# Load order, bias mask, extra small matmuls and delayed sums in a two-block transformer kernel

## The chip, the core and the metric

The kernel runs on one core of a Trainium2 chip. A core has TensorE (PE, matrix products), VectorE (DVE), ScalarE (ACT), GpSimd (POOL) and SyncE (SP, which here only issues transfers), each with a queue of its own, and 16 DMA engines that move data between the chip's memory (HBM) and the on-chip memory. PSUM, in eight banks, takes TensorE's results. The metric is the device time of one execution in microseconds (us); lower is better.

## The reference

One token sequence of 256 rows by 2048 columns, float32, passes through two blocks. What the change touches lies in the first, and in a product that is computed for the second beside it:

```python
def rms_norm(x, g):
    y = xf * lax.rsqrt(jnp.mean(xf * xf, axis=-1, keepdims=True) + NORM_EPS)
    return (y * g).astype(x.dtype)

# first block
xn = rms_norm(h, pre_mix_norm)
proj = xn @ w_in                                   # 2048 x 4608
qa, ka = axial_rope(rms_norm(qa, q_norm)), axial_rope(rms_norm(ka, k_norm))
out_a = global_gqa(qa, ka, va)                     # 8 heads, softmax over 256 keys
out_b = neighbourhood_attn(qb, kb, vb, rel_pos_bias, rows)
    # 8 heads; a key counts only inside a window of 16 columns of a 64-wide grid;
    # scores + rel_pos_bias[head, row distance, column distance]
mix = concat([out_a, out_b]) @ w_o
h = h + rms_norm(mix, post_mix_norm)
m = square(relu(rms_norm(h, pre_mlp_norm) @ w_up)) @ w_down      # 2048 x 8192 x 2048
h = h + rms_norm(m, post_mlp_norm)
...
# second block, first lines
mod = silu(c) @ w_mod + b_mod                      # 2048 x 12288, one row
mod_c = silu(c_ctx) @ w_mod + b_mod
```

The second block then applies a context projection, a gated recurrence, a convolution branch and another MLP of the same size.

## The kernel before

**Pieces and slots.** Every large product streams its weights in pieces of 256 x 512 (512 KB). SP loads a piece into one of four slots of `raw` (`load`, L556: it waits until the low part of the piece four earlier is done). ScalarE writes its rounded high part `whi` (`split`, L641: it waits for the landing, and until TensorE is done with the piece four earlier). VectorE subtracts and writes the low part `wlo` (`split`, L1735). TensorE multiplies each piece in 12 matmuls of 128 x 512 (high x high, high x low, low x high for two halves of the rows and two of the tokens; `chunk`, L1262, the matmul in L1281). The 12 matmuls of a piece are called a slot here, and eight slots a chunk, which fills 512 columns of the result. ScalarE and VectorE work three pieces ahead of TensorE. Between the pieces each engine does other work, which hand-written tables (`extra`, `inserts`) bind to a slot: the same slot number in each engine's own loop.

**Start.** `k_small` holds an identity matrix (`ident`) and ones. TensorE turns (transposes through `ident`) the first gain vector (`turn_vectors`, L1290), then x in eight groups (`x_turn`, L1256); ScalarE and VectorE make high and low parts of each group with the gain applied (`x_high`, `x_low`). Each group's PSUM bank is free again after its low part. The first product is `w_in`, with nine chunks (0 to 8).

**Loads beside the weights.** SP's queue holds, in the order of the program: `k_small`, the first gain, the weight pieces, after piece 4 fourteen small vectors (`vector_loads`), after piece 8 the rotary tables and column mask (`k_early` to `early`), 64 copies of the bias table in HBM (`bias_rows`), and the head gains `q_norm`, `k_norm` broadcast to all partitions (`gqk`), then in chunks 2 and 3 two of the 32 bias loads into `bm` after each piece. ScalarE's queue loads x in two halves.

**Bias mask.** When all of `bm` has landed, GpSimd adds the column mask to it in one operation over 128 x 4096 elements (L2410). VectorE uses `bm` in the attention that follows `w_in`. In chunks 4 to 7 VectorE also normalises and rotates the heads (`rotate`).

**Modulation.** `silu(c) @ w_mod` is not done in slots of its own. VectorE multiplies a piece of `w_mod` by a column of `silu(c)` and adds it to `macc` (L1927, L1930), eight pieces to a block of 512 columns, for c alone or for both c and c_ctx. When the eighth is in, TensorE sums `macc` over the partitions by small matmuls with ones (`mod_sum`, L1386; in the trace 8 for one vector and 16 for both). A plan (`MOD_PLAN`, `AT`) says in which slots of the `w_o` product and of both MLPs the pieces are taken; `MOD_AT` holds them, `SUM_AT` the sums:

```python
SUM_AT.setdefault((name, (a + 1) // 8), {})[(a + 1) % 8] = n_sum   # a: slot of the eighth piece
```

There are three buffers of `macc`; the first product of a block waits for the sum of the block three before. `mod_of_mixer` and `mixer_gains` on VectorE read the finished sums.

## Time and profile before

| | us |
|---|---|
| three runs, median (lowest to highest) | 2971.78 (2967.68 to 2972.05) |
| the profiled execution | 2973.79 |
| its span, first to last instruction | 2972.0 |
| TensorE busy in it | 2857.4 (96%) |
| VectorE, ScalarE, GpSimd busy | 2014.7, 1355.9, 146.9 |
| mean granted TensorE clock | 0.982 of full speed |

TensorE's matmuls overlap, so its busy share counts neighbouring matmuls without a gap. The granted clock has two levels, 1.2 and 2.4 GHz; 1.00 in a row is the higher one throughout. An idle time in brackets at the end of a row is that of the engine just before the operation, with what ended it.

### The profile page before, as it was taken

The numbers are of one execution on the slowest core, as the hardware profiler recorded it, in microseconds if no ns is written. First come the engines' busy times: TensorE is split into PE (matmuls) and PEld (weight loads), VectorE is DVE, ScalarE is ACT, GpSimd is POOL, SyncE is SP. The second block draws the span as 40 slices with busy tenths as digits, with TensorE's granted clock in tenths as the row PEclk, the third lists the DMA queues.
The fourth block names the chain that finished last, engine by engine and source line by source line (L and its number), as shares of the span: only waits on it lengthen the run. The fifth ranks groups of instructions, "written<-read, shape, count | busy, mean of one in ns | idle before, by whom it ended". The sixth has DMA issues, their size and how long they took to land.

```text
span 2972.0 us, 34985 instructions
## 1 busy us (share of the span) xinstructions
PE 2857.4 (96%) x13258; PEld 2370.4 (80%) x13258; DVE 2014.7 (68%) x2263; ACT 1355.9 (46%) x1633; POOL 146.9 (5%) x103
## 2 busy tenths in 40 slices
PE   7998999999999999999999999989979999999997
PEld 6786787888888887787788888888857888888886
DVE  4665779799789787776686487575557754544554
ACT  4446354444443454555444444653434444344442
POOL 0100001010010100000000000000000001010000
PEclk9999999999999999999999999999989999999998
DMA  7661878987878988555666666405547876665653
GB/s 227 198 195 51 277 255 282 320 266 271 286 258 285 324 287 276 177 184 177 202 184 193 194 188 182 131 1 184 190 144 241 275 220 185 193 189 191 188 188 120
DMA packets 322668, 622.52 MB, mean 209 GB/s; under 512 B 27415, under 2 KB 29591, under 8 KB 320919
## 3 DMA queue, kind: packets, MB, share of 16 engines
q1 hardware_dynamic: 319015, 597.96, 63.1%
q10 hardware_dynamic: 3504, 22.55, 2.0%
q8 instruction: 97, 1.59, 0.2%
q14 instruction: 52, 0.43, 0.0%
HBM read 614.14 MB, written 7.24 MB: 209 GB/s over the span
## 4 chain that ended last, share of the span: by engine, by line
PE 83%; DVE 9%; issue 3%; DMA 3%; ACT 2%; SPq 0%; DVEq 0%; POOL 0%; ACTq 0%; POOLq 0%
PE ps L1281 77%; DVE macc L1930 3%; DVE wlo L1741 2%; DMA raw<-w_in 2%; PE ps L1386 1%; PE ps L1256 1%; ACT whi L648 1%; PE ps L1428 1%; PE ps L1646 1%; DVE tcol L2051 1%; PE ps L1628 1%; PE ps L1608 1%; DMA raw<-w_up 0%; DMA raw<-w_o 0%; PE ps L1357 0%
## 5 line engine op out<-in xcount | busy, mean ns | idle before, releaser
L1741 DVE TENSOR_TENSOR wlo<-raw,whi 128x1024 fp32r<-128x1024 f32 x940 | 1171.9, 1252 | 812.0 <-ACT whi L648 807.5
L648 ACT ACTIVATE whi<-raw 128x1024 fp32r<-128x1024 f32 x940 | 995.8, 1060 | 1312.1 <-PE ps L1281 1222.1
L1281 PE MATMUL ps<-whi,hhi 128*128 128x512 f32 x2064 | 811.7, 393 | 1.7 <-DVE hlo L2057 1.2
L1281 PE MATMUL ps<-whi,hlo 128*128 128x512 f32 x2064 | 804.7, 390 | 0.0
L1281 PE MATMUL ps<-wlo,hhi 128*128 128x512 f32 x2064 | 804.3, 390 | 0.0
L1281 PE MATMUL ps<-whi,xhi 128*128 128x512 f32 x1632 | 649.6, 398 | 21.0 <-DVE wlo L1741 16.4
L1281 PE MATMUL ps<-wlo,xhi 128*128 128x512 f32 x1632 | 642.2, 393 | 0.0
L1281 PE MATMUL ps<-whi,xlo 128*128 128x512 f32 x1632 | 641.8, 393 | 0.0
L1281 PEld LDWEIGHTS ps<-whi,hhi 128*128 128x128 f32 x2064 | 388.2, 188 | 83.4 <-DVE hlo L2057 3.1
L1281 PEld LDWEIGHTS ps<-whi,hlo 128*128 128x128 f32 x2064 | 388.0, 188 | 81.6
L1281 PEld LDWEIGHTS ps<-wlo,hhi 128*128 128x128 f32 x2064 | 388.3, 188 | 79.5 <-issue 1.0
L1281 PEld LDWEIGHTS ps<-whi,xhi 128*128 128x128 f32 x1632 | 311.2, 191 | 89.3 <-DVE wlo L1741 14.5
L1281 PEld LDWEIGHTS ps<-whi,xlo 128*128 128x128 f32 x1632 | 310.6, 190 | 66.0
L1281 PEld LDWEIGHTS ps<-wlo,xhi 128*128 128x128 f32 x1632 | 311.2, 191 | 62.9
L1930 DVE SCALAR_TENSOR_TENSOR macc<-mraw,stat,macc 128x512 f32<-128x512 f32 x480 | 350.4, 760 | 4.5
L2428 POOL TENSOR_TENSOR sqrow<-rrow 128x512 f32<-128x512 f32 x64 | 95.2, 1508 | 1192.7 <-ACT rrow L825 1192.7
L2211 DVE SCALAR_TENSOR_TENSOR yT<-uT,cols,yT 128x252 f32<-128x252 f32 (+17 forms) x144 | 52.9, 431 | 0.0
L2403 POOL TENSOR_TENSOR stat<-stat 128x2 f32<-128x2 f32 x11 | 10.8, 985 | 818.0 <-DVE stat L1759 283.2
L1996 DVE TENSOR_TENSOR yrow<-ps,yrow 128x512 f32<-128x512 f32 x48 | 30.9, 686 | 24.2 <-PE ps L1281 24.2
L1628 PE MATMUL ps<-qD,kD 128*128 128x128 f32 x256 | 35.9, 284 | 7.2 <-DVE qD L2287 6.3
L1386 PEld LDWEIGHTS ps<-small,macc 128*128 128x128 f32 x256 | 33.4, 202 | 11.5 <-DVE macc L1930 10.5
L1990 DVE TENSOR_TENSOR hlo<-ps,hhi 128x512 fp32r<-128x512 f32 x64 | 41.0, 682 | 0.0
(280 smaller groups left out, 1548.0 us busy)
## 6 DMA issues: line engine op xcount, KB each, us to landing
raw<-w_in SPq DMA_DIRECT2D x296, 512.0 KB, 4.3
raw<-mlp_w SPq DMA_DIRECT2D x256, 512.0 KB, 3.7
mraw<-w_mod SPq DMA_DIRECT2D x192, 512.0 KB, 6.1
raw<-w_up SPq DMA_DIRECT2D x128, 512.0 KB, 5.1
raw<-w_down SPq DMA_DIRECT2D x128, 512.0 KB, 5.3
raw<-w_o SPq DMA_DIRECT2D x32, 512.0 KB, 5.8
raw<-w_ple_gate SPq DMA_DIRECT2D x32, 512.0 KB, 4.2
raw<-w_out SPq DMA_DIRECT2D x32, 512.0 KB, 4.3
```

The lines of the kernel that those rows point to most:

```text
L648: nc.scalar.activation(whi[:, s % NSLOT], raw[:, s % NSLOT], ACT.Copy).then_inc(hi_done, 1)
L1256: ins = nc.tensor.transpose(ps[:, TB[t % 2], c:c + P], src, ident)
L1281: ins = nc.tensor.matmul(ps[:, bank(par) + th], a[:, kt, th * P:(th + 1) * P], b[:, (s + u) % NSLOT, k], start=(kt == 0 and m == 0), stop= ...
L1386: ins = nc.tensor.matmul(ps[:, MB, n * 8 + 2 * b + v:n * 8 + 2 * b + v + 1], macc[:, v, m % 3, b * P:(b + 1) * P], ones[:, 0:1], start=Tru ...
L1428: ins = nc.tensor.transpose(ps[:, TB[(t0 + h) % 2], a * T + th * P:a * T + (th + 1) * P], sqrow[:, th, f:f + P], ident)
L1628: ins = nc.tensor.matmul(o[:, (2 * hh + n) * P:(2 * hh + n + 1) * P], k[:, hh, n * P:(n + 1) * P], q[:, hh, t * P:(t + 1) * P], start=True ...
L1741: nc.vector.tensor_tensor(wlo[:, s % NSLOT], raw[:, s % NSLOT], whi[:, s % NSLOT].bitcast(F32), ALU.subtract)\
L1930: ins = nc.vector.scalar_tensor_tensor(out=a, in0=w, scalar=x, in1=a, op0=ALU.mult, op1=ALU.add)
L1990: nc.vector.tensor_tensor(hlo[:, kt:kt + 2], ps[:, TB[(t0 + h) % 2]].rearrange("p (a b) -> p a b", a=2), hhi[:, kt:kt + 2].bitcast(F32), A ...
L1996: ins = nc.vector.tensor_tensor(y, ps[:, bank(g) + th], y, ALU.add)
L2211: nc.vector.scalar_tensor_tensor(out=y, in0=tap_part(uT[:, ct], ct, dd, True), scalar=wcol(TAPS // 2 + dd, ct), in1=y, op0=ALU.mult, op1=A ...
L2428: nc.gpsimd.tensor_tensor(sqrow[:, th], rrow[:, th], rrow[:, th], ALU.mult).then_inc(sq_done, 1)
```

## The change

- **First loads.** SP loads x's first half, piece 0, x's second half and the other pieces, in this order. `k_small` and the first gain go to ScalarE's queue.
- **First splits.** ScalarE and VectorE treat the first group of x before piece 0, not after it.
- **Small matmuls.** TensorE issues 12 matmuls of `ident` by `ident` into an unused PSUM bank after the turn of the first gain, and 6 after the second turn of x (`keep_running`). Nobody reads them.
- **Tables spread.** Bias rows after piece 10, head gains after piece 16, `early` after piece 24; the 32 bias loads in chunks 4 and 5.
- **Bias mask.** Off GpSimd; on VectorE in eight operations of 128 x 512, one per slot of chunk 8. Attention waits for all eight.
- **Sums.** `SUM_AT` puts a sum three slots behind its eighth piece (in the `w_o` product at most in its last slot, 31, so its second sum stays where it was). `mod_of_mixer` moves from slot 1 to 4 and `mixer_gains` from 4 to 6 of chunk 24 of the first MLP. The last sum of that MLP falls behind its last chunk, where the program already issued any such sum.

ScalarE, from the start of the program. Before:

```order
L677 DMA res<-x 128x2x1024 x2
L648 ACT_TABLE_LOAD [waits landed0]
L648 ACTIVATE whi<-raw 128x1024 [waits vec_cols]
L687 ACTIVATE xhi<-ps,cols 128x256 [waits t_done]
L687 ACTIVATE xhi<-ps,cols 128x256
```

With the change:

```order
L685 DMA small<-k_small 128x256
L686 DMA vecs<-pre_mix_norm 16x128
L694 ACT_TABLE_LOAD [waits t_done]
L694 ACTIVATE xhi<-ps,cols 128x256 [waits vec_cols]
L694 ACTIVATE xhi<-ps,cols 128x256
L657 ACTIVATE whi<-raw 128x1024 [waits landed0]
```

The table load now waits for the first turn of x, no longer for piece 0.

TensorE, from the start, with the change (before, the turns of x followed the first row directly):

```order
L1297 MATMUL ps<-small,vecs 128x16 [waits gain_in,small_in]
L1321 MATMUL ps<-small 128x128 x12
L1263 MATMUL ps<-small,res 128x128 [waits x_in0]
L1263 MATMUL ps<-small,res 128x128 x3
L1263 MATMUL ps<-small,res 128x128 [waits x_in0]
L1263 MATMUL ps<-small,res 128x128 x3
L1321 MATMUL ps<-small 128x128 x6
L1263 MATMUL ps<-small,res 128x128 [waits t_free,x_in0,acc_free]
```

The 12 stand ahead of the first turn of x.

SP, behind the small vectors (pieces 5 and on). Before:

```order
L560 DMA raw<-w_in 128x2x512 [waits lo_done] x4
L549 DMA early<-k_early 128x576
L550 DMA bias_rows<-rel_pos_bias 64x3720
L551 DMA gqk<-q_norm 128x8x128
L553 DMA gqk<-k_norm 128x2x128
L560 DMA raw<-w_in 128x2x512 [waits lo_done] x8
L577 DMA bm<-bias_rows 64x4x64 [waits bias_copied]
```

With the change:

```order
L566 DMA raw<-w_in 128x2x512 [waits lo_done] x6
L551 DMA bias_rows<-rel_pos_bias 64x3720
L566 DMA raw<-w_in 128x2x512 [waits lo_done] x6
L554 DMA gqk<-q_norm 128x8x128
L556 DMA gqk<-k_norm 128x2x128
L566 DMA raw<-w_in 128x2x512 [waits lo_done] x8
L560 DMA early<-k_early 128x576
L566 DMA raw<-w_in 128x2x512 [waits lo_done] x8
L583 DMA bm<-bias_rows 64x4x64 [waits bias_copied]
```

The head gains now stand between pieces 16 and 17, alone.

TensorE in chunk 3 of the first MLP, around the fourth sum (sqrow: the turn of the hidden rows in slot 3; "..." stands for the other eleven matmuls of a slot). Before:

```order
L1428 MATMUL ps<-small,sqrow 128x128 x3
L1281 MATMUL ps<-whi,xhi 128x512 [waits lo_done]
...
L1281 MATMUL ps<-whi,xhi 128x512 [waits lo_done]
...
L1386 MATMUL ps<-small,macc 128x1 [waits m_mul]
L1386 MATMUL ps<-small,macc 128x1 x7
L1281 MATMUL ps<-whi,xhi 128x512 [waits lo_done]
```

With the change:

```order
L1441 MATMUL ps<-small,sqrow 128x128 x3
L1288 MATMUL ps<-whi,xhi 128x512 [waits lo_done]
...
L1288 MATMUL ps<-whi,xhi 128x512 [waits lo_done]
...
L1288 MATMUL ps<-whi,xhi 128x512 [waits lo_done]
...
L1288 MATMUL ps<-whi,xhi 128x512 [waits lo_done]
...
L1399 MATMUL ps<-small,macc 128x1 [waits m_mul]
L1399 MATMUL ps<-small,macc 128x1 x7
L1288 MATMUL ps<-whi,xhi 128x512 [waits lo_done]
```

The sum stood before slot 5 of the chunk and now stands before slot 7.

The diff:

```diff
--- before.py
+++ after.py
@@ -469,7 +469,8 @@
                     MOD_AT.setdefault((name, a // 8), {})[a % 8] = len(MODQ)
                     MODQ.append((n, r, n_sum, 2 if both else 1, n_ops))
                     n_ops += 4 if both else 2
-                SUM_AT.setdefault((name, (a + 1) // 8), {})[(a + 1) % 8] = n_sum
+                a = min(a + 3, 31) if name == "o" else a + 3
+                SUM_AT.setdefault((name, a // 8), {})[a % 8] = n_sum
                 n_sum += 1
                 if both:
                     n_ctx_sums = n_sum
@@ -527,8 +528,9 @@
 
         @block.sync
         def _(sp):
-            sp.dma_start(small[:], I["k_small"]).then_inc(small_in, 16)
-            sp.dma_start(vecs[0:KT, 0, :], I["pre_mix_norm"][0].rearrange("(b p) -> b p", p=P)).then_inc(gain_in, 16)
+            def half_tokens(h):
+                sp.dma_start(res[:, :, h * (D // 2):(h + 1) * (D // 2)],
+                             rows_of(I["x"][0])[:, :, h * (D // 2):(h + 1) * (D // 2)]).then_inc(x_in[h], 16)
 
             def vector_loads():
                 for gi, group in enumerate(VEC_GROUPS):
@@ -545,13 +547,17 @@
                         sp.dma_start(vecs[r:r + rows, gi, :], src).then_inc(vec_in, 16)
                         r += rows
 
-            def attention_loads():
-                sp.dma_start(early[:], I["k_early"]).then_inc(early_in, 16)
+            def bias_rows_out():
                 sp.dma_start(bias_rows, bass.AP(I["rel_pos_bias"].tensor, 0, [[0, GRID], [1, NB]])).then_inc(bias_copied, 16)
+
+            def head_gains():
                 sp.dma_start(gqk[:, 0:A_Q * HD].rearrange("p (h d) -> p h d", d=HD),
                              bass.AP(I["q_norm"].tensor, 0, [[0, P], [0, A_Q], [1, HD]])).then_inc(gqk_in, 16)
                 sp.dma_start(gqk[:, A_Q * HD:].rearrange("p (h d) -> p h d", d=HD),
                              bass.AP(I["k_norm"].tensor, 0, [[0, P], [0, A_KV], [1, HD]])).then_inc(gqk_in, 16)
+
+            def tables():
+                sp.dma_start(early[:], I["k_early"]).then_inc(early_in, 16)
 
             def load(src, p, s):
 
@@ -582,11 +588,14 @@
                 bias_load(n)
                 bias_load(n + 1)
 
-            chunk(w_in, 0, 0, extra={4: vector_loads})
-            chunk(w_in, 8, NCH, extra={0: attention_loads})
-            for c in (2, 3):
-                chunk(w_in, 8 * c, c * NCH, extra={u: (lambda n=16 * (c - 2) + 2 * u: two_biases(n)) for u in range(8)})
-            with sp.Fori(4, IN1 // NCH) as i:
+            half_tokens(0)
+            chunk(w_in, 0, 0, extra={0: lambda: half_tokens(1), 4: vector_loads})
+            chunk(w_in, 8, NCH, extra={2: bias_rows_out})
+            chunk(w_in, 16, 2 * NCH, extra={0: head_gains})
+            chunk(w_in, 24, 3 * NCH, extra={0: tables})
+            for c in (4, 5):
+                chunk(w_in, 8 * c, c * NCH, extra={u: (lambda n=16 * (c - 4) + 2 * u: two_biases(n)) for u in range(8)})
+            with sp.Fori(6, IN1 // NCH) as i:
                 chunk(w_in, i * 8, i * NCH)
             def mod_load(q):
                 n, r, _, _, _ = MODQ[q]
@@ -673,10 +682,8 @@
                                                scale=gain[:, 2 * g + j:2 * g + j + 1])
                 ins.then_inc(t_hi, 1)
 
-            for h in range(2):
-                act.dma_start(res[:, :, h * (D // 2):(h + 1) * (D // 2)],
-                              rows_of(I["x"][0])[:, :, h * (D // 2):(h + 1) * (D // 2)]).then_inc(x_in[h], 16)
-
+            act.dma_start(small[:], I["k_small"]).then_inc(small_in, 16)
+            act.dma_start(vecs[0:KT, 0, :], I["pre_mix_norm"][0].rearrange("(b p) -> b p", p=P)).then_inc(gain_in, 16)
             gain0 = col("pre_mix_norm")
 
             def x_high(g):
@@ -707,8 +714,8 @@
 
             p0, g0 = plan["in"]
             act.wait_ge(vec_cols, 1)
+            x_high(0)
             split(0, 0)
-            x_high(0)
             x_high(1)
             split(1, 1)
             x_high(2)
@@ -1309,9 +1316,15 @@
             p0, g0 = plan["in"]
             pe.wait_ge(small_in, 16)
             pe.wait_ge(gain_in, 16)
+            def keep_running(count):
+                for n in range(count):
+                    nc.tensor.matmul(ps[:, 7, 0:P], ident, ident, start=True, stop=True)
+
             turn_vectors(0, 1)
+            keep_running(12)
             x_turn(0)
             x_turn(1)
+            keep_running(6)
             chunk(p0, g0, xhi, xlo, inserts={u: (lambda u=u: x_part(u)) for u in range(8)})
             chunk(p0 + 8, g0 + 1, xhi, xlo, inserts={2: other_vectors})
             chunk(p0 + 16, g0 + 2, xhi, xlo)
@@ -1814,8 +1827,8 @@
             assert n0 == 0
             dve.wait_ge(vec_turned, 1)
             nc.vector.tensor_copy(cols[:, 0:KT], ps[:, MB, 0:KT]).then_inc(vec_cols, 1)
+            x_low(0)
             split(0, 0)
-            x_low(0)
             x_low(1)
             split(1, 1)
             x_low(2)
@@ -1866,6 +1879,15 @@
                     nc.vector.tensor_tensor(pj, ra, rb, ALU.add).then_inc(rope_done, 1)
                     dve.wait_ge(rope_done, n + 1)
                 return dict(enumerate([squares, mean_squares, norm_heads, gain, by_cos, lambda: by_sin(0), lambda: by_sin(1), total]))
+
+            def column_mask(u):
+                if u == 0:
+                    dve.wait_ge(bias_in, 16 * ROWS * B_H)
+                    dve.wait_ge(early_in, 16)
+                n = TH * B_H * ROWS // 8
+                b3 = bm[:].rearrange("p t h (a b) -> p (t h a) b", b=GRID)[:, n * u:n * u + n]
+                nc.vector.tensor_tensor(b3, b3, colmask.unsqueeze(1).to_broadcast([P, n, GRID]), ALU.add).then_inc(bias_done, 1)
+            in_extra[8] = {u: (lambda u=u: column_mask(u)) for u in range(8)}
 
             p0, g0 = plan["in"]
             for c in range(IN1 // NCH):
@@ -1902,7 +1924,7 @@
                 nc.vector.tensor_tensor(xlo[:, HEAD_KT[i]], ps[:, 6 + i % 2, 0:T], xhi[:, HEAD_KT[i]].bitcast(F32), ALU.subtract)\
                     .then_inc(o_lo, 1)
 
-            dve.wait_ge(bias_done, 1)
+            dve.wait_ge(bias_done, 8)
             for i in range(NHEAD + 3):
                 if i < NHEAD:
                     score_max(i)
@@ -2065,7 +2087,7 @@
             d_first = c_first + 32
             context_col = lambda g: mod_col("normc", g, mcol[:, 1], modT[:, 0:KT, 1])
             mlp("mlp1", place({0: lambda: post0_res(3), 1: low1(3), 2: low1(4), 3: low1(5), 4: low1(6), 5: low1(7), 6: norm1_mean_square,
-                               c_first + 1: mod_of_mixer, c_first + 4: mixer_gains,
+                               c_first + 4: mod_of_mixer, c_first + 6: mixer_gains,
                                d_first + 8: context_mean_square, d_first + 10: lambda: scaled_row("normc", trow, trow),
                                d_first + 14: lambda: context_col(0),
                                **{d_first + 16 + 2 * g: (lambda g=g: [mod_low("normc", g, xhi, xlo), context_col(g + 1)]) for g in range(7)},
@@ -2404,11 +2426,6 @@
 
             pool.wait_ge(half_set, 1)
             rstd("norm0")
-            pool.wait_ge(bias_in, 16 * ROWS * B_H)
-            pool.wait_ge(early_in, 16)
-            b3 = bm[:].rearrange("p t h (a b) -> p (t h a) b", b=GRID)
-            nc.gpsimd.tensor_tensor(b3, b3, colmask.unsqueeze(1).to_broadcast([P, TH * B_H * ROWS, GRID]), ALU.add)\
-                .then_inc(bias_done, 1)
             for n in range(4):
                 pool.wait_ge(qk_ss, n + 1)
                 nc.gpsimd.tensor_tensor(stat[:, 24:24 + SET], stat[:, 16:16 + SET], stat[:, 128:128 + SET], ALU.pow)\
```

## Rows read from the trace of the kernel before

**Rows 1.** The page: span; busy time, share and instructions of each engine.

```profile
span 2972.0 us, 34985 instructions
PE 2857.4 (96%) x13258; PEld 2370.4 (80%) x13258; DVE 2014.7 (68%) x2263; ACT 1355.9 (46%) x1633; POOL 146.9 (5%) x103
```

**Rows 2.** VectorE's timeline: start, duration, operation, [idle before it].

```profile
131.25 0.82 DVE L1856 TENSOR_TENSOR rota<-proj,early 128x640 f32<-128x640 f32 x1
...
216.92 1.23 DVE L1741 TENSOR_TENSOR wlo<-raw,whi 128x1024 fp32r<-128x1024 f32 x1 [1.49 <-ACT whi L648]
```

**Rows 3.** Who waited for whom, whole span: us in total, times, longest.

```profile
PE ps L1281 <- DVE wlo L1741: 16.4, 8, 4.5
...
PE ps L1386 <- DVE macc L1930: 6.5, 5, 3.9
```

**Rows 4.** Busy time by stretch, granted clock, DMA.

```profile
core 0: us, PE busy (x) PEld busy (x) DVE busy (x) ACT busy (x) POOL busy (x), PEclk, DMA share, GB/s
50.00:60.00 10.00, 9.49 (x34) 7.60 (x35) 5.27 (x5) 5.99 (x7) 0.00 (x0) 0.76 0.83 259
60.00:80.00 20.00, 20.00 (x90) 16.53 (x90) 9.86 (x9) 8.93 (x11) 0.00 (x0) 1.00 0.88 234
100.00:120.00 20.00, 17.29 (x71) 13.88 (x70) 15.27 (x6) 6.33 (x6) 9.03 (x1) 0.91 0.52 166
338.00:346.00 8.00, 8.00 (x26) 6.49 (x26) 1.18 (x2) 1.56 (x5) 0.00 (x0) 0.57 0.76 277
492.00:499.00 7.00, 7.00 (x25) 6.24 (x26) 5.88 (x8) 0.00 (x0) 0.00 (x0) 0.53 0.85 256
868.00:875.00 7.00, 6.95 (x32) 5.58 (x31) 5.08 (x7) 1.06 (x1) 0.00 (x0) 0.76 0.81 278
```

**Rows 5.** Timeline of the start, all engines.

```profile
8.38 1.97 PE L1256 MATMUL ps<-small,res 128*128 128x128 f32 x8
...
11.98 1.28 ACT L648 ACT_TABLE_LOAD   x1 [11.98 <-DMA raw<-w_in]
...
14.24 1.55 ACT L687 ACTIVATE xhi<-ps,cols 128x256 fp32r<-128x256 f32 x4
...
17.26 0.78 PE L1281 MATMUL ps<-whi,xhi 128*128 128x512 f32 x1
```

**Rows 6.** DMA issues, 0 to 120 us: KB each, us to landing.

```profile
gqk<-q_norm SPq DMA_DIRECT2D x1, 512.0 KB, 19.1
...
vecs<-pre_mix_norm SPq DMA_DIRECT2D x1, 8.0 KB, 6.9
```

**Rows 7.** Timelines around three sums: TensorE, and VectorE before the second.

```profile
336.76 2.31 PE L1386 MATMUL ps<-small,macc 128*128 128x1 f32 x16 [0.84 <-DVE macc L1930]
...
486.85 2.34 DVE L1741 TENSOR_TENSOR wlo<-raw,whi 128x1024 fp32r<-128x1024 f32 x2
...
491.90 3.58 PE L1386 MATMUL ps<-small,macc 128*128 128x1 f32 x16 [3.87 <-DVE macc L1930]
...
868.65 1.95 PE L1386 MATMUL ps<-small,macc 128*128 128x1 f32 x16
```

**Rows 8.** Timeline, 29 to 51 us: SP, ScalarE, TensorE.

```profile
29.13 27.31 SPq L560 DMA_DIRECT2D raw<-w_in  x8
...
48.15 1.06 ACT L648 ACTIVATE whi<-raw 128x1024 fp32r<-128x1024 f32 x1 [9.30 <-DMA raw<-w_in]
...
50.51 0.80 PE L1281 MATMUL ps<-whi,xhi 128*128 128x512 f32 x1 [4.47 <-DVE wlo L1741]
```

**Rows 9.** DMA rate from 30 to 50 us, in 40 steps of 0.5 us.

```profile
GB/s 431 446 446 476 115 44 19 31 41 45 32 27 45 43 42 45 20 41 45 41 44 46 17 38 45 36 34 23 48 73 133 280 410 414 418 377 406 381 410 385
```

**Rows 10.** Timeline of GpSimd and TensorE around the bias mask.

```profile
103.30 9.03 POOL L2410 TENSOR_TENSOR bm<-bm,early 128x4096 f32<-128x4096 f32 x1 [61.82 <-DMA bm<-bias_rows]
...
113.47 0.80 PE L1281 MATMUL ps<-whi,xhi 128*128 128x512 f32 x1 [2.71 <-DVE wlo L1741]
```

**Rows 11.** Chain of work that ended last, 100 to 120 us: start, us, what.

```profile
103.78 9.64 DVE wlo L1741
```


## The prediction

> **What bounds the kernel now.** I read the page's busy shares first, then who waited for whom, then the timeline where the change works. TensorE is busy 96% of a span of 2972.0 us [rows 1], in steps of one 512 KB weight piece (a "slot" of 12 matmuls, 2.72 us: one split of 1.23 us on VectorE plus the 1.49 us that it then sits idle [rows 2]). Nothing that leaves those matmuls alone can win more than the idle and slow-clock time around them, so I priced only that. TensorE waited 16.4 us in 8 waits for the low part of a piece and 6.5 us in 5 waits for a modulation product [rows 3]. The granted clock tells a second price: in a stretch the time lost at the lower level is its width times (1 minus the mean granted clock). That is 10 x 0.24 = 2.4 us in 50 to 60, 20 x 0.09 = 1.8 us in 100 to 120, 8 x 0.43 = 3.4 us in 338 to 346, 7 x 0.47 = 3.3 us in 492 to 499 and 7 x 0.24 = 1.7 us in 868 to 875 [rows 4]. Each follows one of the waits or sums below.
>
> **Start.** Before, the two halves of x and four weight pieces share the DMA engines, the table load waits until piece 0 lands at 11.98, and split, x parts and low parts follow one another to the first product at 17.26 [rows 5]. The change puts x and the weights in one queue in the order of use, and k_small and the first gain in ScalarE's. The new chain does not begin at piece 0 but at that gain, which landed 6.9 us after its issue [rows 6], just ahead of the turns at 8.38 [rows 5]. Then come the 12 new matmuls, which are on the path. No row shows them. Above, the turns at the start take 1.97 / 8 = 0.25 us each [rows 5], so 3.0 us in all; below, the 16 small matmuls of a sum take 1.95 us, 0.12 each, so 1.5 us [rows 7]. With 0.25 (they start after an idle stretch like those turns): turn of the gain to 8.5, 12 matmuls to 11.5, four turns (1.0) to 12.5, table load (1.28) to 13.8, the first pair of high parts (1.55 / 2) to 14.6, split (1.06, as ScalarE's of any piece) to 15.6, low part (1.23) to 16.9: 0.4 us earlier than 17.26. With 0.12 it is 1.9 us earlier. A gain vector that is alone in its queue could land up to 3 us sooner, or the 12 matmuls could cost more than they fill; I take **1.5 us**, between -1 and +5. The matmuls may also lift the clock before the first slot, which runs slow now (up to 1.8 us, the price of the slow stretch after 113); there are still gaps of a microsecond in between, so I count **0.5 us**. The six matmuls after the second turn stand before a wait for VectorE and cost nothing; if that wait were gone, 0.7 to 1.5 us.
>
> **Tables spread.** At 50.51 TensorE stood 4.47 us, and ScalarE 9.30 us for the landing of piece 9 [rows 8]. That piece was issued at 29.13 behind both head gains [rows 8], which take 19.1 us to land [rows 6]; from 32.5 to 44.5 the DMA engines move 17 to 48 GB/s in every half microsecond, from 46 on 400 again [rows 9]. So the broadcast of the gains blocks the queue for 13 us, piece 9 lands 3.1 us after its end (48.1), and 2.4 us later TensorE starts. That is 18.5 us after the gains begin to move, then, against 14.0 us from their begin (32.0) to the need at 50.51 - 4.47 = 46.0: 4.5 us late, as seen. Stall and slow clock (2.4 us, less 0.3 of it inside the stall: 2.1) cost 6.6 us. The change does not take the broadcast away; it puts it after piece 16, with the bias rows no longer before it. It should begin 2 to 3.5 us after its issue, which is 19.5 us before piece 17 is needed (a piece's own lead of 46.0 - 29.1 = 16.9 us, and one slot). That gives 16.0 to 17.5 us where 18.5 are wanted: 1.0 to 2.5 us of stall, now at piece 17, plus about 1.5 us of slow clock behind it. I take 2.0 + 1.5 = 3.5 us, a **gain of 3.1 us** (0 if the stall stays as it is, 6.6 if it goes). Bias rows and the tables, alone among pieces, hide in the same lead. The 32 bias loads go from chunks 2 and 3 to 4 and 5: 60 to 80 shows what they cost beside the weights, TensorE 20.00 of 20.00 with DMA at 0.88 [rows 4], so nothing; SP's pieces queue behind them as before. The new cover is VectorE's rotation, which takes 0.82 us of its 1.49 idle us [rows 2]; without that cover every late piece would be seen.
>
> A rule weighs against this part. The trace says that the 512-byte packets of the broadcast crawl [rows 9]. The Trainium skill, page "DMA: Bandwidth & Descriptors", section Specifications, gives 512 B or more as the smallest transfer for line rate; by that the two gains would pass in about 2 us, the bytes ahead of piece 9 would be to blame, and spreading them would win all 6.6 us. The row decides for me; the rule's case is the third rival.
>
> **Bias mask.** GpSimd's one addition over 4096 elements runs 103.30 to 112.33, and TensorE then waits 2.71 us for VectorE [rows 10]: the split that began at 103.78 lasted 9.64 us [rows 11] in place of 1.23. With the 1.8 us of slow clock, less 0.3 inside the stall, that is **4.2 us**, and it goes entirely. The eight additions of 512 elements on VectorE stand in chunk 8, after the bias loads: 0.82 us for 640 elements [rows 2] makes 0.66 each, 5.3 in all, inside an idle of 1.49 us per slot. Nothing is queued behind them but the splits, three slots ahead of TensorE. If an eighth took GpSimd's rate (1.13 us) it would still fit. Between 3 and 4.5 us.
>
> **Sums two slots later.** A sum of 8 or 16 matmuls stood one slot behind its last product, and TensorE waited for that product although the next piece was ready. At 336.76 it waited 0.84 and lost 3.4 us of clock; at 491.90 it waited 3.87 and lost 3.3 [rows 4, 7]. Two more slots are 5.4 us of room, more than any wait. All five waits go: 6.5 us [rows 3]. The last, about 0.5, is not won: the pieces after it wait for a DMA. At 491.90 VectorE is itself full, and TensorE soon needs its next low part: 0.4 us come back. The clock losses behind the two long ones (6.7) go as well, since there is no idle stretch before them. **12.3 us.** I leave the 1.7 us behind the sum at 868.65 out, which came after 1.95 us of small matmuls and no wait to speak of [rows 4, 7]: the same may now strike one sum of another phase, so it neither goes nor comes. Ends: 5 us (waits alone, part of them found again as waits for low parts) and 15 us. The mixer's modulation and gains, moved by three and two slots on VectorE, are four short operations with a chunk to spare: nothing. No product waits for a later sum, since its buffer is asked for two groups on.
>
> A rule that bears on the 6.7 us: by the Trainium skill, page "TensorE: Matmul & The Clock Gate", section Part 1: The HAM clock gate, the number of slow matmuls at a start differs between runs of the same kernel. By that the 6.7 could be anything from 0 to 8; the first rival has its lower end.
>
> **Sum.** 1.5 + 0.5 + 3.1 + 4.2 + 12.3 = 21.6 us. The profiled execution took 2973.79 us, 2.0 above the median of 2971.78, so 2952.2 for it and **2950.2 for the median**; I say 2950.
>
> **Rivals.**
> 1. The clock does not come back and the start gains nothing: the 16 small matmuls themselves bring the lower level, as at 868.65, wherever they stand. For it: that row. Against: of the six sums of that length that waited under 0.1 us, only that one shows it. 21.6 - 6.7 - 2.0 = 12.9 us: 2959. Chance 0.2.
> 2. The waits for sums turn into waits for low parts, because VectorE is full in 484 to 492. For it: it works without a pause there. Against: two low parts lay ready from 489.2 on [rows 7]. The 3.87 and 3.3 us are lost: 14.4 us, 2957. Chance 0.08.
> 3. The broadcast is not what holds piece 9; its stall goes whole, and the early gain comes 3 us sooner: 21.6 + 3.5 + 3 = 28.1 us, 2944. For it: by bytes alone the queue would be empty at once. Against: [rows 9]. Chance 0.13.
> 4. Slower: the bias loads in chunks 4 and 5 meet the rotation. DMA is busy at 0.88 there and a slot's loads fill the slot; if they took 4.5 us in place of 2.7, sixteen slots would lose 29 us and outweigh the gains: 2979. It decides from 1.4 us lost a slot on (21.6 / 16), with nothing else failing. Against it: the same bytes in 60 to 80 delay nobody. Chance 0.02.
> 5. The change works only in part and ends within 0.2% (about 6 us, what a measurement of this kernel can tell from no change): 0.04.
>
> The forecast itself has 0.53, from 2946 to 2956. The range for 8 in 10 takes in most of rivals 1 to 3: 2942 to 2960. Faster by over 0.2% (below 2965.8): 0.94; within: 0.04; slower: 0.02.
>
> **What would show it.** First product between 14 and 17 us, and its spacing tells the clock. A stall of 1 to 2.5 us at the second piece of chunk 2, none at piece 9. No split above 1.3 us near 103, and eight additions of about 0.66 us with no wait on TensorE in the last chunk. No wait of a sum for macc anywhere, and a full granted clock behind 340 and 490. The forecast is wrong if a stall of over 5 us stands at piece 17, if the waits on macc return as waits on wlo, or if the start moves past 18 us.

## The result, and the profile after

| | before | with the change |
|---|---|---|
| median of four runs each, us | 2969.73 (2966.61 to 2972.05) | 2947.93 (2947.61 to 2951.75) |
| ratio of the times | | 0.9929, interval 0.9914 to 0.9945 |
| profiled execution, us | 2973.79 | 2947.61 |
| its span, us | 2972.0 | 2945.7 |

The change is worth 21.8 us, with an interval of 16 to 26; 21.6 were forecast. The two traces differ by more, 26.3 us of span, because the profiled execution of before is 4.1 us above its median of four, and that of after 0.3 below its own.

The page of the changed kernel: span, and busy time of each engine, to be held against [rows 1].

```profile
span 2945.7 us, 35013 instructions
...
PE 2845.1 (97%) x13294; PEld 2364.0 (80%) x13294; DVE 2013.6 (68%) x2271; ACT 1355.3 (46%) x1633; POOL 139.9 (5%) x102
```

TensorE has 36 matmul records more, two for each of the 18 small matmuls, and is yet busy 12.3 us less: that part was time at the lower clock. The other 14 of the 26.3 us of span are idle time of TensorE that is gone. GpSimd gives up 7 us, VectorE takes eight more instructions.

Who waited for whom in the changed kernel (us in total, times, longest), against [rows 3]:

```profile
PE ps L1288 <- DVE wlo L1754: 13.7, 9, 5.3
```

There is no row of TensorE waiting for macc at L1399 any more (before 6.5 us in 5 waits). Waits for low parts fell from 16.4 to 13.7 us only, because new ones came.

Busy time and granted clock by stretch (columns as in [rows 4]) of the changed kernel. The last three are the stretches around the sums that stood at 336.76, 491.90 and 868.65 before; all work there now comes 12 to 23 us earlier.

```profile
18.00:22.00 4.00, 4.00 (x12) 3.13 (x11) 4.00 (x6) 2.58 (x4) 0.00 (x0) 0.57 0.52 148
44.00:54.00 10.00, 10.00 (x47) 8.12 (x46) 3.76 (x4) 5.16 (x6) 0.00 (x0) 1.00 0.65 207
60.00:80.00 20.00, 17.77 (x78) 14.36 (x78) 7.84 (x7) 7.54 (x10) 0.00 (x0) 1.00 0.67 224
100.00:120.00 20.00, 20.00 (x90) 16.57 (x89) 10.96 (x12) 8.58 (x9) 2.08 (x1) 1.00 0.86 231
326.00:334.00 8.00, 8.00 (x45) 6.92 (x44) 6.87 (x9) 4.33 (x7) 0.00 (x0) 1.00 0.87 301
479.00:486.00 7.00, 7.00 (x40) 6.10 (x40) 6.93 (x10) 2.44 (x3) 0.00 (x0) 1.00 0.86 271
852.00:859.00 7.00, 7.00 (x40) 6.11 (x39) 6.41 (x8) 2.75 (x3) 3.06 (x2) 1.00 0.80 277
```

Each stretch that ran at 0.53 to 0.91 in [rows 4] is at 1.00, with one new loss at 18 to 22. The 40 matmul records in seven microseconds (25 before, at 492) say the same.

**Where the time went.** A difference between two traces can be split by the start of the same piece on TensorE in both timelines. Pieces are counted from 0 within each product, "chunk 4, piece 1" from 0 within the chunk:

| first matmul of | before | after | ahead by | what lies between |
|---|---|---|---|---|
| piece 0 | 17.26 | 17.70 | -0.44 | the start |
| piece 10 | 56.06 | 49.68 | 6.38 | stall at piece 9 and slow clock: +6.82 |
| piece 18 | 77.95 | 74.16 | 3.79 | new stall at piece 17: -2.59 |
| chunk 4, piece 1 | 123.09 | 114.96 | 8.13 | bias mask: +4.34 |
| `w_o`, piece 2 | 293.27 | 284.01 | 9.26 | attention, clock at other places: +1.13 |
| first MLP, chunk 24, piece 1 | 969.24 | 946.17 | 23.07 | sums: +13.81 |
| last piece | 2945.69 | 2919.43 | 26.26 | the rest: +3.19 |

The last row is not a work of the change. It is made of places where the lower clock falls in one trace and not in the other, and of a wait for a transfer in the context projection that takes back about a microsecond.

### The profile page after: what moved, and what is told of

It is laid out like the page before. It is cut to its first block, busy times and chain, and to the rows that moved or that the text cites. A ratio compares the mean times of both kernels' runs of the same rounds, so it can differ in the third digit from the quotient of the medians.

```text
span 2945.7 us, 35013 instructions
## 1 busy us (share of the span) xinstructions
PE 2845.1 (97%) x13294; PEld 2364.0 (80%) x13294; DVE 2013.6 (68%) x2271; ACT 1355.3 (46%) x1633; POOL 139.9 (5%) x102
## 4 chain that ended last, share of the span: by engine, by line
PE 87%; DVE 6%; DMA 3%; issue 2%; ACT 2%; DVEq 0%; SPq 0%; POOL 0%; ACTq 0%; POOLq 0%
PE ps L1288 81%; DVE wlo L1754 1%; DMA raw<-w_in 1%; DVE macc L1952 1%; PE ps L1441 1%; PE ps L1263 1%; PE ps L1399 1%; DMA raw<-w_up 1%; ACT whi L657 1%; PE ps L1641 1%; PE ps L1621 1%; DVE tcol L2073 1%; PE ps L1659 1%; DMA raw<-w_o 0%; PE ps L1370 0%
## 5 line engine op out<-in xcount | busy, mean ns | idle before, releaser
L1288 PE MATMUL ps<-whi,xhi 128*128 128x512 f32 x1632 | 645.1, 395 | 18.3 <-DVE wlo L1754 13.7
L1141 ACT ACTIVATE dec<-ps 128x1024 f32<-128x1024 f32 x32 | 32.4, 1027 | 17.0 <-PE ps L1621 15.1
```

The source lines that it names most:

```text
L1141: nc.scalar.activation(dst, src, ACT.Exp).then_inc(d_done, 1)
L1288: ins = nc.tensor.matmul(ps[:, bank(par) + th], a[:, kt, th * P:(th + 1) * P], b[:, (s + u) % NSLOT, k], start=(kt == 0 and m == 0), stop= ...
```

## The experiments

All were timed beside runs of the kernel before on the same chip, 4 to 11 runs each. Mask alone, mask and tables, sums alone and the change without small matmuls share one series of the kernel before (median 2970.03, 15 runs), the other four a second one on another chip (2969.21, 15 runs). The change itself was timed in a third one.

| kernel | median us | ratio to before | interval |
|---|---|---|---|
| mask alone, on before | 2964.78 | 0.998 | 0.997 to 0.9989 |
| mask and tables spread, on before | 2962.04 | 0.9972 | 0.996 to 0.9984 |
| sums alone, on before | 2955.49 | 0.9948 | 0.9934 to 0.9961 |
| the change without small matmuls | 2943.26 | 0.9903 | 0.9888 to 0.9918 |
| mask in eight parts, still on GpSimd | 2966.62 | 0.9989 | 0.998 to 0.9998 |
| the change, sums two slots behind | 2950.19 | 0.9928 | 0.9915 to 0.9942 |
| the change, head gains in five transfers | 2946.2 | 0.9919 | 0.9905 to 0.9932 |
| the best of these together | 2938.2 | 0.9889 | 0.9874 to 0.9905 |

### The mask alone, and the mask in eight parts on GpSimd

Kernel before, with the change's `column_mask` on VectorE only:

```diff
+            in_extra[8] = {u: (lambda u=u: column_mask(u)) for u in range(8)}
...
-            dve.wait_ge(bias_done, 1)
+            dve.wait_ge(bias_done, 8)
...
-            nc.gpsimd.tensor_tensor(b3, b3, colmask.unsqueeze(1).to_broadcast([P, TH * B_H * ROWS, GRID]), ALU.add)\
-                .then_inc(bias_done, 1)
```

> The kernel before with the bias mask alone moved to VectorE, in eight parts in chunk 8. My theory: GpSimd's 9.03 us addition held VectorE's split (9.64 us in place of 1.23), so both the 2.71 us wait of TensorE near 113 and the 1.5 us of slow clock behind it go: 4.3 us less, no split above 1.3 us near 103, eight additions of 0.66 us. Rival: the split was long because its high part or a transfer was late, and then a long split stays near 103 and nothing is won. A second rival, that VectorE's extra 5.3 us in chunk 8 delay low parts, would give a wait of TensorE after 207.

And the rival form: the addition stays on GpSimd, but cut into eight (VectorE waits for all eight, as above):

```diff
-            nc.gpsimd.tensor_tensor(b3, b3, colmask.unsqueeze(1).to_broadcast([P, TH * B_H * ROWS, GRID]), ALU.add)\
-                .then_inc(bias_done, 1)
+            for u in range(8):
+                n = TH * B_H * ROWS // 8
+                nc.gpsimd.tensor_tensor(b3[:, n * u:n * u + n], b3[:, n * u:n * u + n], colmask.unsqueeze(1).to_broadcast([P, n, GRID]), ALU.add)\
+                    .then_inc(bias_done, 1)
```

> The kernel before with the bias mask still on GpSimd, but cut into eight additions of 512 elements. My theory: a VectorE split that meets a GpSimd addition waits until that one ends; the whole one took 9.03 us, an eighth some 1.1 to 1.3, so a split takes at most 2.5 us, VectorE's lead of 5.6 us covers it, and TensorE's wait near 113 goes: 1.7 to 4.3 us less, as with the mask on VectorE. Rival: it is the total of GpSimd's work beside VectorE that counts, or GpSimd's eight parts follow each other so closely that a split waits for several; then a split of over 7 us and a wait of TensorE stay.

The mask alone gave 5.3 us by the medians (2970.03 - 2964.78), with an interval of 3 to 9 us; its trace gives 2.88 + 1.45 = 4.33 between the same pieces. With eight parts on GpSimd it was 2.6 us by the medians (2969.21 - 2966.62), with an interval of 0.6 to 5.9, and 4.33 by the trace too. VectorE's timeline of the changed kernel, in the last chunk of `w_in`, shows what it costs:

```profile
202.87 0.68 DVE L1889 TENSOR_TENSOR bm<-bm,early 128x512 f32<-128x512 f32 x1
203.47 1.22 DVE L1754 TENSOR_TENSOR wlo<-raw,whi 128x1024 fp32r<-128x1024 f32 x1
204.61 0.68 DVE L1889 TENSOR_TENSOR bm<-bm,early 128x512 f32<-128x512 f32 x1
206.07 1.23 DVE L1754 TENSOR_TENSOR wlo<-raw,whi 128x1024 fp32r<-128x1024 f32 x1 [0.78 <-ACT whi L657]
```

The addition takes 0.68 us and the split behind it still waits for its high part: it fits. With eight parts on GpSimd, the timeline of GpSimd and VectorE reads:

```profile
102.45 14.99 POOL L2412 TENSOR_TENSOR bm<-bm,early 128x512 f32<-128x512 f32 x8 [61.15 <-DMA bm<-bias_rows]
...
108.48 2.07 DVE L1741 TENSOR_TENSOR wlo<-raw,whi 128x1024 fp32r<-128x1024 f32 x1 [1.42 <-ACT whi L648]
111.20 1.59 DVE L1741 TENSOR_TENSOR wlo<-raw,whi 128x1024 fp32r<-128x1024 f32 x1 [0.65 <-ACT whi L648]
113.92 2.36 DVE L1741 TENSOR_TENSOR wlo<-raw,whi 128x1024 fp32r<-128x1024 f32 x1 [1.13 <-ACT whi L648]
116.21 1.92 DVE L1841 TENSOR_TENSOR rota<-proj 128x640 f32<-128x640 f32 x1
```

Splits last up to 2.36 us in place of 1.23, but none 9.64 as in [rows 11], and TensorE does not wait. GpSimd pays too: the same 4096 elements take 14.99 us where the single operation took 9.03 [rows 10]. So the two engines hold each other up, each for about the rest of the other's operation (a split of at most 1.23 + 9.03 / 8 = 2.36 us), and what hurts TensorE is the length of the single operation, not the engine that has it.

The Trainium skill, page "SBUF — State Buffer", section "SBUF: two separate sides", says that VectorE, in an operation with two inputs in SBUF as the split is, and a GpSimd operation that reads SBUF share a pair of ports as an exclusive lock held for the whole instruction. The rows agree. Even the order in time fits: in the kernel with the sums alone, the split was there first.

```profile
103.98 1.23 DVE L1742 TENSOR_TENSOR wlo<-raw,whi 128x1024 fp32r<-128x1024 f32 x1 [1.49 <-ACT whi L649]
104.58 9.55 POOL L2411 TENSOR_TENSOR bm<-bm,early 128x4096 f32<-128x4096 f32 x1 [63.17 <-DMA bm<-bias_rows]
...
106.71 8.50 DVE L1742 TENSOR_TENSOR wlo<-raw,whi 128x1024 fp32r<-128x1024 f32 x1 [1.50 <-ACT whi L649]
```

There the first split ran its normal 1.23 us, GpSimd's operation took 9.55 in place of 9.03, and the next split was held for 8.50. TensorE then waited 1.59 us, at 115.27, and its clock stayed at 1.00 from 100 to 120. Between piece 18 and chunk 4, piece 1, this comes to 1.9 us in this trace and 4.3 in that of before, so the price of the mask varies between traces. That it varies with where in a slot the addition begins is likely, but two traces don't show it.

### The tables spread, beside the mask

```diff
-            chunk(w_in, 8, NCH, extra={0: attention_loads})
-            for c in (2, 3):
-                chunk(w_in, 8 * c, c * NCH, extra={u: (lambda n=16 * (c - 2) + 2 * u: two_biases(n)) for u in range(8)})
-            with sp.Fori(4, IN1 // NCH) as i:
+            chunk(w_in, 8, NCH, extra={2: bias_rows_out})
+            chunk(w_in, 16, 2 * NCH, extra={0: head_gains})
+            chunk(w_in, 24, 3 * NCH, extra={0: tables})
+            for c in (4, 5):
+                chunk(w_in, 8 * c, c * NCH, extra={u: (lambda n=16 * (c - 4) + 2 * u: two_biases(n)) for u in range(8)})
+            with sp.Fori(6, IN1 // NCH) as i:
```

(and the edits of the mask kernel). The spread was not tried without the mask: with the bias loads in chunks 4 and 5, GpSimd would wait for them ahead of the steps that the rotation in chunk 4 needs, while the loads wait for the pieces behind that rotation.

> The mask on VectorE and the tables spread as in the change; start and sums as before. Against the mask alone this shows the spreading: my theory gives 6.8 us won at piece 9 (4.6 wait, 2.2 slow clock) and 2.2 to 2.4 us lost at piece 17, where the head gains now stand in front; so about 4.4 us less than the mask alone, 8.7 less than before. Rival: the gain at piece 9 needs the new start too (x and weights in one queue), and then a wait of some us stays at piece 9.

2962.04, 2.7 us below the mask alone, where 4.4 were expected; the intervals of the two ratios overlap. Its trace has the 4.63 and 2.15 us won at pieces 9 and 10, so the new start is not needed for them, and a new wait of 1.49 us at piece 17 (69.20). From piece 8 to 18 the traces give 4.9 us against the mask alone; why the medians show less was not traced. In the changed kernel the same wait at piece 17 is 2.23. Its path runs through three timelines; SP, ScalarE and TensorE:

```profile
49.30 0.47 SPq L554 DMA_DIRECT2D gqk<-q_norm  x1
49.81 0.97 SPq L556 DMA_DIRECT2D gqk<-k_norm  x1
...
68.90 1.06 ACT L657 ACTIVATE whi<-raw 128x1024 fp32r<-128x1024 f32 x1 [9.58 <-DMA raw<-w_in]
...
71.27 0.50 PE L1288 MATMUL ps<-whi,xhi 128*128 128x512 f32 x1 [2.23 <-DVE wlo L1754]
```

and the DMA rate of the changed kernel from 48 to 75 us (40 steps of 0.675 us), with the share of time in which its DMA engines were busy, in tenths, and the time to landing of the gains:

```profile
DMA  4795677312210111331122222499999987317896
GB/s 46 246 394 149 146 303 266 105 54 49 56 56 24 44 42 45 28 35 39 42 55 70 84 74 83 149 322 387 408 361 361 355 340 285 143 33 146 313 337 164
...
gqk<-q_norm SPq DMA_DIRECT2D x1, 512.0 KB, 16.8
gqk<-k_norm SPq DMA_DIRECT2D x1, 128.0 KB, 17.7
```

From 53 to 65 us the DMA engines again move 24 to 84 GB/s, and piece 17 lands behind it at 68.9. So the broadcast itself is slow, wherever it stands, as the prediction read from [rows 9]. The engines were busy under four tenths of that time, mostly one or two: in the DMA records of the trace a 512-byte packet of the broadcast holds its engine for 25 ns in the median and a 2048-byte packet of a weight piece for 84, so the time goes between the packets and not in them. What the move changed is how early it is issued against the need.

### The head gains in five transfers

The changed kernel, with the broadcast cut by heads and spread over pieces:

```diff
-            chunk(w_in, 16, 2 * NCH, extra={0: head_gains})
-            chunk(w_in, 24, 3 * NCH, extra={0: tables})
+            chunk(w_in, 16, 2 * NCH, extra={u: (lambda n=u // 2: head_gains(n)) for u in (0, 2, 4, 6)})
+            chunk(w_in, 24, 3 * NCH, extra={0: lambda: head_gains(4), 2: tables})
...
-                        dve.wait_ge(gqk_in, 32)
+                        dve.wait_ge(gqk_in, 80)
```

`head_gains(n)` loads two heads: those of `q_norm` for n from 0 to 3, those of `k_norm` for 4.

> The changed kernel with the head gains' broadcast cut into five transfers of two heads each, after pieces 16, 18, 20, 22 and 24. My theory: it is the number of 512-byte packets in one go (1280, 13 us at about 40 GB/s) that outlasts the lead of the next piece; a fifth takes 2.6 us and hides, and the 2.23 us wait at piece 17 goes: 2.2 to 2.4 us less than the changed kernel, no wait on low parts between 60 and 90 us. Rival: each transfer of that kind has a fixed long time to land, and then pieces 17, 19, 21, 23 and 25 come late and waits stay or add up. By bytes alone (640 KB at 400 GB/s) there would be nothing to spread in the first place.

2946.2, against 2947.93 for the change (in another series: the ratios are 0.9919 and 0.9929, with intervals that overlap). By the traces, piece 17 gave 2.6 us between pieces 1 and 18. TensorE has no wait for a piece from 19 to 219 us, and the stretch of 60 to 80 is full:

```profile
60.00:80.00 20.00, 20.00 (x90) 16.57 (x89) 8.58 (x7) 9.65 (x11) 0.00 (x0) 1.00 0.81 220
```

The DMA issues from 50 to 90 us, with KB each and median us to landing:

```profile
raw<-w_in SPq DMA_DIRECT2D x14, 512.0 KB, 5.1
gqk<-q_norm SPq DMA_DIRECT2D x3, 128.0 KB, 5.9
...
gqk<-k_norm SPq DMA_DIRECT2D x1, 128.0 KB, 7.1
```

A fifth of the broadcast lands in 5.9 or 7.1 us, next to 5.1 for a piece. Each part delays the queue by less than the lead of the pieces behind it, so TensorE does not see it. The sum of the bytes and the number of packets are the same as in one go.

The Trainium skill, page "DMA: Bandwidth & Descriptors", section Specifications, names 512 B as the size from which transfers reach line rate. The rows differ: while the broadcast's 512-byte packets went through, the DMA engines moved about 40 GB/s in both traces, beside about 400 GB/s for pieces. Here the measurement decides. The third rival is refuted: the stall came back at piece 17. Whether it is the size of the packets that leaves the gaps between them, or that all of them read the same few hundred bytes, was not tested.

### The small matmuls

```diff
             turn_vectors(0, 1)
-            keep_running(12)
             x_turn(0)
             x_turn(1)
-            keep_running(6)
```

> The changed kernel without its 18 small matmuls at the start. My theory: the 12 before the first turn of x take 4.5 us on the path (8.04 to 12.5) and buy nothing, since the clock falls again at 18.5 before the first slot is through; without them the turns start at 8.0, the table load at 9.1, and the first product at 13.3 to 13.7 in place of 17.7, its slot still slow (4.6 us): 4.0 to 4.4 us less. Rival one: piece 0 or x lands too late and takes their place, and under 2 us are won. Rival two: the small matmuls kept the clock up for part of the first slots, and without them another 1.8 us are lost there.

2943.26, 4.7 us below the change's 2947.93 (in another series, with intervals of the ratios that barely overlap). TensorE's timeline of the start, with the change:

```profile
7.86 0.25 PE L1297 MATMUL ps<-small,vecs 16*128 16x16 f32 x1 [7.86 <-DMA vecs<-pre_mix_norm]
8.04 4.64 PE L1321 MATMUL ps<-small 128*128 128x128 f32 x24
...
12.53 1.04 PE L1263 MATMUL ps<-small,res 128*128 128x128 f32 x8
...
17.70 0.47 PE L1288 MATMUL ps<-whi,xhi 128*128 128x512 f32 x1 [0.67 <-DVE wlo L1754]
```

with the gains in five transfers, whose start is the same program:

```profile
7.86 5.42 PE L1320 MATMUL ps<-small 128*128 128x128 f32 x24
...
13.12 1.04 PE L1262 MATMUL ps<-small,res 128*128 128x128 f32 x8
...
18.29 0.47 PE L1287 MATMUL ps<-whi,xhi 128*128 128x512 f32 x1 [0.67 <-DVE wlo L1753]
```

and without the small matmuls:

```profile
7.89 0.25 PE L1297 MATMUL ps<-small,vecs 16*128 16x16 f32 x1 [7.89 <-DMA vecs<-pre_mix_norm]
8.07 1.97 PE L1263 MATMUL ps<-small,res 128*128 128x128 f32 x8
...
13.76 0.77 PE L1288 MATMUL ps<-whi,xhi 128*128 128x512 f32 x1 [0.21 <-DVE wlo L1752]
```

The 12 issued matmuls are 24 in the trace. The x8 of the turns is not doubled: it covers both groups, and eight turns are issued. So a turn leaves one record and a plain matmul of the same float32 shape two. The records start 0.21 us apart at the low clock and 0.11 at the high one. With the change the clock rose after 16 of the 24 and the turns start 4.46 us later than without them; in the kernel with the gains in five all 24 were slow (5.26 us), and so they were in the one with the sums two slots behind (5.28 us). The first product comes at 17.70, 18.29 and 18.97 us in these three, against 13.76 without.

What the clock gives in return is not the same each time either. With the change, the first slot began at the high clock (matmuls 0.23 us apart), fell to the low one at 18.5 (0.43 apart, the row of 18 to 22 with 0.57) and needed 4.76 us up to the first matmul of piece 1; before it was 4.81. In the other two the slot kept the high clock and needed 3.16 and 3.20 us. So the slot gained up to 1.6 us where the small matmuls had cost 0.8 more. Piece 1 tells the balance: it began at 22.46 with the change, at 21.45 and 22.17 in those two, and at 18.83 without the small matmuls, 2.6 to 3.6 us sooner. (The clock column shows 1.00 for the start of a trace whatever the spacing, so there the spacing has to be read.)

The Trainium skill, page "TensorE: Matmul & The Clock Gate", section "Part 1: The HAM clock gate", says that the number of slow matmuls at a start varies between runs of one kernel. These three traces agree, as far as kernels that only start alike can: 16 of the 24 records were slow in one, all 24 in the other two.

### The sums

Sums alone, on the kernel before:

```diff
-                SUM_AT.setdefault((name, (a + 1) // 8), {})[(a + 1) % 8] = n_sum
+                a = min(a + 3, 31) if name == "o" else a + 3
+                SUM_AT.setdefault((name, a // 8), {})[a % 8] = n_sum
...
-                               c_first + 1: mod_of_mixer, c_first + 4: mixer_gains,
+                               c_first + 4: mod_of_mixer, c_first + 6: mixer_gains,
```

> The kernel before with the sums alone three slots behind their products (and the mixer's two steps with them). My theory: the waits for macc go (6.5 us) and with them the slow clock behind the sums at 336, 491 and 868 (3.0, 3.2 and 1.7 us); VectorE gives about 1.1 us back as two short waits for low parts in chunk 3 of the first MLP, and the last sum's 0.9 us are lost in a transfer behind it. 12 to 14 us less than before, as in the changed kernel. Rival: the clock losses went in the changed kernel only because the phase of the whole program was shifted by the earlier parts; then one or more slow stretches stand behind sums here, and the gain is 5 to 9 us.

2955.49: 14.5 us. The rival of the prediction was that the small matmuls of a sum bring the lower clock wherever they stand, that of this run that the earlier parts of the change had taken the slow spells away by shifting the program. Both are refuted by the granted clock over the same stretches of `w_o` and the first MLP. Before, with the sums one slot behind (columns as in [rows 4]):

```profile
325.00:450.00 125.00, 123.93 (x556) 102.10 (x556) 96.41 (x116) 60.65 (x84) 5.32 (x4) 0.96 0.79 262
450.00:500.00 50.00, 45.32 (x206) 37.66 (x205) 46.43 (x58) 18.18 (x22) 5.89 (x4) 0.93 0.85 286
```

the sums alone:

```profile
325.00:450.00 125.00, 124.76 (x586) 103.67 (x585) 99.89 (x121) 63.37 (x88) 8.88 (x6) 1.00 0.82 275
450.00:500.00 50.00, 49.52 (x239) 41.24 (x238) 49.82 (x60) 21.10 (x24) 5.58 (x4) 1.00 0.87 296
```

0.96 over 125 us is 5 us of lost time, 0.93 over 50 is 3.5. The second is gone, and the first but for some 1.5 us of a spell that began at 324.53 and in the other trace lies ahead of the stretch, at 321.0. In all four kernels with sums one slot behind (that of before among them) the clock fell three or four times between 325 and 1130 us; in the five with sums three slots behind, and in the one with two, never. In all four it fell around the fourth sum, which waited 3.8 to 3.9 us. Elsewhere it is not regular. At the first sum it fell in three of them, behind waits of 0.84, 0.86 and 2.44 us, and not in the fourth, the mask in eight parts on GpSimd, whose first sum waited 0.86 as well:

```profile
326.00:340.00 14.00, 13.14 (x66) 10.88 (x66) 10.01 (x13) 5.39 (x8) 0.00 (x0) 1.00 0.74 266
```

The spell behind the 16 small matmuls at 868.65 [rows 7] is not fixed to that place: in the other three kernels with sums one slot behind it stands between 630 and 682, each time behind a sum of 16 that hardly waited.

How much room is needed was tried by taking a slot back, in the changed kernel:

```diff
-                a = min(a + 3, 31) if name == "o" else a + 3
+                a = min(a + 2, 31) if name == "o" else a + 2
```

> The changed kernel with its sums two slots behind their products in place of three. My theory: one slot less is 2.7 us less room, so of the sums only the fourth (chunk 3 of the first MLP), which waited 3.87 us at one slot, still waits: about 0.8 to 1.2 us, with perhaps 1.6 to 3.3 us of slow clock behind it; all others none. 1 to 4 us more than the changed kernel. Rival: the wait was never for the product but for the order of sum and pieces, and then two slots give the same trace as three.

2950.19, not told apart from the change (ratios 0.9928 and 0.9929). TensorE's timeline around the fourth sum, the one that cost most before:

```profile
474.65 0.50 PE L1288 MATMUL ps<-whi,xhi 128*128 128x512 f32 x1 [0.77 <-DVE wlo L1754]
478.44 1.95 PE L1399 MATMUL ps<-small,macc 128*128 128x1 f32 x16 [0.77 <-DVE macc L1952]
```

Where the sum waited 3.87 us one slot behind [rows 7], it waits 0.77 two slots behind and nothing three slots behind. The clock stays at 1.00 from 325 to 1130 as well, so the 1.6 to 3.3 us of slow clock that the expectation thought possible did not come. The second slot brings nearly all of it; the third takes away a wait of less than a microsecond. Near the start, behind a stall of 2.06 us at piece 17, the clock fell in this trace for 3.4 us, which it did not do with the change:

```profile
72.00:76.00 4.00, 4.00 (x12) 3.11 (x12) 2.37 (x3) 2.70 (x4) 0.00 (x0) 0.57 0.82 250
```

### The best version

From the change: no small matmuls, gains in five, and the table load taken off the path by a copy of one column at ScalarE's start:

```diff
+            act.wait_ge(half_set, 1)
+            nc.scalar.activation(stat[:, 155:156], stat[:, 128:129], ACT.Copy)
```

> The changed kernel without its 18 small matmuls, with the head gains in five transfers, and with ScalarE's table load taken out of the chain by a tiny copy at its start. My theory: 3.9 us for the small matmuls, 2.3 us for piece 17, and 1.3 us for the table load, which now runs while the first gain is under way: 7.5 us less than the changed kernel, first product at 12.4 to 12.8. Rival: with the table load gone the chain waits for piece 0 to land (8.97 in the changed kernel) or for VectorE, and under 1 us of the 1.3 is won.

2938.2 (2937.47 to 2938.85): 31 us below before (2969.21) and 9.7 below the change (in another series), where 7.5 were expected. Its start:

```profile
1.74 1.28 ACT L687 ACT_TABLE_LOAD   x1 [1.74 <-issue]
...
9.18 0.84 ACT L695 ACTIVATE xhi<-ps,cols 128x256 fp32r<-128x256 f32 x2 [5.94 <-PE ps L1264]
...
12.37 0.76 PE L1289 MATMUL ps<-whi,xhi 128*128 128x512 f32 x1 [0.20 <-DVE wlo L1753]
...
12.83 1.06 ACT L656 ACTIVATE whi<-raw 128x1024 fp32r<-128x1024 f32 x1 [1.14 <-DMA raw<-w_in]
```

The table load stands at 1.74 instead of 13.21. The first product comes 1.4 us before that of the kernel that only lacks the small matmuls (13.76) and 5.3 us before that of the change, and the next thing to be late is piece 1 on the DMA. Of the 9.7 us, 5.3 are that start and about 2.6 piece 17; the remaining 1.8 were not traced to a place.

## Why the prediction was right, point by point

The time, 2950 against 2947.93, was right, and so were three of its four steps. One had the wrong sign, and two errors of size made up for it. Of the 2.3 us between 2950.2 and 2947.93, 2.05 come from the base: the fourth run of the kernel before moved its median from 2971.78 to 2969.73.

- **Start: wrong.** The prediction counted +1.5 and +0.5 us; the trace gives -0.44, within the first term's bound of -1. The step that failed is the price of the 12 small matmuls. It was put at 3.0 us by the rate of the turns, 1.97 / 8, and at 1.5 by that of a sum's rows, 1.95 / 16, both multiplied by the 12 issued. But each of them stands in the trace as two records, so 12 cost 4.5 us here and 5.3 in two other traces. A turn leaves one record, so its rate could not be carried over; and the doubling was in sight in the sum, which has 8 matmuls in the order of instructions and x16 in the timeline. The rest of the chain came about as taken: the gain was there at 7.86, and from the first turn to the first product it took 5.2 us where 5.4 were counted. The clock term came out at zero in this trace; in two others the first slot was 1.6 us shorter, but the small matmuls before it 0.8 longer. Without them the first product came at 13.76, 3.5 us earlier than before. The six after the second turn stood before a wait for VectorE (1.50 us) and cost nothing, as forecast.
- **Tables spread: right in kind, 1.2 us too small.** Piece 9 gave 6.8 us (6.6 forecast). The new stall at the second piece of chunk 2 came where it was expected, 2.2 us long (2.0 forecast; 1.5, 1.8 and 2.1 in three other kernels). But the 1.5 us of slow clock behind it did not come: 60 to 80 reads 1.00. Net 4.2 instead of 3.1. It did come in one of those three, the one with the sums two slots behind (stall of 2.06 us): its row of 72 to 76 us has 0.57. So the term is missed in this trace and not excluded in general. No bias load in chunks 4 and 5 delayed a piece (8.13 ahead at chunk 4, and still 8.13 at chunk 5), so the fourth rival is out.
- **Bias mask: right.** 4.3 us against 4.2, 0.68 us an eighth against 0.66. The doubt that remains is about before: the same addition cost 1.9 us in the trace of the sums alone.
- **Sums: right in kind, 1.5 us too small.** 13.8 us against 12.3. By how far the changed kernel is ahead behind and before each sum, the one at 336.76 gave 13.55 - 9.24 = 4.3 (0.84 + 3.4 forecast), the one at 491.90 gave 20.29 - 14.14 = 6.15 with one new wait for a low part in it (0.75, 0.4 forecast). The 1.7 us of clock behind 868.65, which the prediction left out, came as well (about 1.9). The second rival, waits that turn into waits for low parts, holds for 1.1 us only: 0.36 at 471.01 and 0.75 at 474.79. As forecast, pieces after the last sum wait for a DMA: 5.35 us for the low part at 1151.51, where before had 4.37 at 1175.04.
- **The whole.** The rows of the table in the result give -0.4 + 4.2 + 4.3 + 13.8 = 21.9 us, against 21.6 forecast: -2.4, +1.1, +0.1 and +1.5 cancel. From the medians, mask and spread (8.0) and sums (14.5) make 22.5, and the start's -0.4 leaves 22.1 of 21.8 measured. That the errors cancel is luck. The first rival (12.9 us, the clock not coming back) is excluded by the six traces with sums two or three slots behind.

## What to carry to other kernels

Price an instruction that the trace doesn't show by the same kind of instruction elsewhere, and compare its issued count with the rows' count: a plain float32 matmul left two records here, a transpose of the same shape one. Filler in front of work that waits for it is paid in full, and what it gave back in clock was less. When a consumer stands right behind its producer and waits a little, move it by a slot or two: the wait is the smaller part of the gain where TensorE's clock falls behind it (0.84 us of wait and 3.4 of clock at one place, though 0.86 and none in another trace). A slow transfer or a long operation on a shared path is best cut: in pieces shorter than the lead of the work that they block, both the gains and the mask cost TensorE nothing by the traces, and the gains moved as a whole came back at another place.

## What was not expected of the hardware

- An issued float32 matmul of 128 x 128 leaves two records, 0.21 us apart at the low clock and 0.11 at the high one; a transpose of that shape leaves one. The 18 small matmuls at the start put piece 1 off by 2.6 to 3.6 us in three traces, with the first slot 1.6 us shorter in two of them counted in.
- The same stall at piece 17 was followed by no slow clock at 1.49, 1.85 and 2.23 us, and by 3.4 us of it at 2.06. A wait of 0.84 us at 336.76 was followed by it and one of 0.86 with eight parts on GpSimd was not, nor one of 1.59 at 115.27 with the sums alone, while the 16 matmuls of a sum without a wait to speak of at 868.65 were. So the length of the idle time alone doesn't tell whether the clock will fall. What does was not settled here.
- The broadcast of the head gains left the DMA engines idle for over six tenths of its time, in a queue where pieces before and after it ran at about 400 GB/s.
- GpSimd and VectorE slow each other, not only the one that comes second: 4096 elements took GpSimd 9.0 us as one operation and 15.0 us as eight between VectorE's splits.
